# Moving a LayerNorm's mean into the block products that precede it, in a two-layer trunk kernel

## The reference

```python
proj = h @ P['o_w_in'][oi]
bg, cg, xi = proj[..., :512], proj[..., 512:1024], proj[..., 1024:1536]
uv = jax.nn.gelu(proj[..., 1536:])
yc = bg * causal_dwconv(cg * xi, c_conv_w, c_conv_b)
u = uv[..., :512]
v = layernorm(uv[..., 512:], d_ln_g, d_ln_b)      # mean and variance over the 512 channels
mix = einsum('gij,nkjgc->nkigc', tril(d_spatial_w), v in chunks of 128 tokens) + d_spatial_b
yd = u * mix
x = x + gate * (concatenate([yc, yd]) @ P['o_w_out'][oi])
```

## Time and profile before

| | |
|---|---|
| median of 3 runs | 2394.05 us (2391.03 to 2394.49) |
| profiled execution, its own time | 2396.07 us |
| span from its first to its last instruction | 2394.3 us |
| mean granted TensorE clock, of full speed | 0.991 |
| TensorE busy | 2335.9 us (98%) |
| VectorE, ScalarE, GpSimd busy | 1349.8, 749.9, 841.3 us |

### The profile page before, as it was taken

The page is one execution under the profiler, slowest core; times in us unless marked ns, Lnnn a source line. Parts: engine busy times, 40 slices in busy tenths (PEclk is TensorE's granted clock), DMA queues, the critical chain, the costliest instruction groups (busy, mean ns, idle before and its releaser), DMA issues.

```text
span 2394.3 us, 41414 instructions
## 1 busy us (share of the span) xinstructions
PE 2335.9 (98%) x17335; PEld 2223.6 (93%) x17335; DVE 1349.8 (56%) x2663; ACT 749.9 (31%) x1200; POOL 841.3 (35%) x685
## 2 busy tenths in 40 slices
PE   7999999999999999999999999899999999999998
PEld 5997888579999999999999999899999999999998
DVE  5367743466645555445546774556655555544556
ACT  5222234426322222222224523334422222222224
POOL 3221111213344433433333446522444333443341
PEclk9999999999999999999999999999999999999999
DMA  9424343971221222222221211311233434344111
GB/s 309 170 69 134 110 148 102 304 236 36 71 89 56 86 71 80 80 89 86 74 89 54 109 54 50 139 37 36 75 128 124 142 131 145 128 145 145 54 54 73
DMA packets 164566, 258.06 MB, mean 108 GB/s; under 512 B 6228, under 2 KB 150889, under 8 KB 162718
## 3 DMA queue, kind: packets, MB, share of 16 engines
q1 hardware_dynamic: 151370, 187.98, 23.6%
q0 software_dynamic: 4752, 63.28, 7.7%
q10 hardware_dynamic: 8260, 4.15, 0.6%
HBM read 232.36 MB, written 66.86 MB: 125 GB/s over the span
## 4 chain that ended last, share of the span: by engine, by line
PE 76%; DVE 2%; ACT 1%; issue 0%; POOL 0%; ACTq 0%; DVEq 0%
PE ps L3163 24%; PE ps L3192 13%; PE ps L3193 13%; PE ps L3194 13%; PE ps L3359 4%; PE ps L3313 3%; PE ps L3425 2%; PE ps L3511 1%; PE ps L3382 1%; PE ps L3705 0%; DVE tmp L2741 0%; POOL w_slot L2958 0%; DVE h_lo L2363 0%; PE ps L3544 0%; DVE x L2138 0%
## 5 line engine op out<-in xcount | busy, mean ns | idle before, releaser
L2949 POOL TENSOR_TENSOR w_slot<-w_raw,w_slot 128x512 fp32r<-128x512 f32 x272 | 358.7, 1350 | 603.0 <-DVE w_sum L2327 547.7
L3163 PE MATMUL ps<-f_hi,w_slot 128*128 128x352 f32 x1920 | 467.4, 323 | 0.0
L3192 PE MATMUL ps<-h_hi,w_slot 128*128 128x264 f32 x1536 | 437.6, 285 | 0.0
L3193 PE MATMUL ps<-h_lo,w_slot 128*128 128x264 f32 x1536 | 436.5, 284 | 0.0
L3194 PE MATMUL ps<-h_hi,w_slot 128*128 128x264 f32 x1536 | 435.2, 283 | 0.0
L2221 DVE SCALAR_TENSOR_TENSOR x<-ps,mod,x 128x704 f32<-128x704 f32 x368 | 259.2, 746 | 238.3 <-PE ps L3163 227.3
L2958 POOL TENSOR_TENSOR w_slot<-w_sum,w_slot 128x512 fp32r<-128x512 f32 x192 | 248.7, 1329 | 282.9 <-ACT w_slot L1756 282.9
L3163 PE MATMUL ps<-h_hi,w_slot 128*128 128x352 f32 x1296 | 343.3, 331 | 0.3 <-ACT sig L1607 0.3
L3163 PEld LDWEIGHTS ps<-f_hi,w_slot 128*128 128x128 f32 x1920 | 333.7, 188 | 4.1 <-issue 4.1
L3163 PE MATMUL ps<-f_lo,w_slot 128*128 128x352 f32 x960 | 307.8, 321 | 0.0
L3194 PEld LDWEIGHTS ps<-h_hi,w_slot 128*128 128x128 f32 x1536 | 289.5, 189 | 0.0
(11 more groups left out here) (467 smaller groups left out, 4017.8 us busy)
## 6 DMA issues: line engine op xcount, KB each, us to landing
w_raw<-in_ada_w SPq DMA_DIRECT2D x48, 1024.0 KB, 5.4
w_raw<-in_ffn_w_gate_up SPq DMA_DIRECT2D x44, 1024.0 KB, 5.1
out_kv_sample<-in_cache_b_kv POOLq DMA_DIRECT2D x8, 4088.0 KB, 18.4
w_raw<-in_ffn_w_down SPq DMA_DIRECT2D x22, 1024.0 KB, 4.8
w_raw<-in_e_w_in SPq DMA_DIRECT2D x11, 1024.0 KB, 5.5
w_raw<-in_o_w_in SPq DMA_DIRECT2D x10, 1024.0 KB, 5.1
cache<-in_cache_b_kv SPq DMA_DIRECT2D x16, 512.0 KB, 6.3
out_kv_sample<-in_cache_b_kv POOLq DMA_DIRECT2D x8, 1016.0 KB, 6.1
```

Source lines behind the costliest of these rows:

```text
L2949: pool.tensor_tensor(w_slot[slot_of(it.raw)][:, c], w_raw[it.raw.slot][:, c], w_slot[it.hi[0]].bitcast(F32)[:, c], ALU.subtract).then_inc( ...
L3163: mm = pe.matmul(big(t)[:, b, 0:BLK], wt, xt[:, k, b * BLK:b * BLK + BLK], start=(k == 0 and n == 0), stop=(k == K - 1 and n == 2))
L3192: pe.matmul(bank(it, j), w_high, x_high, start=first, stop=False, skip_group_check=True)
L3193: pe.matmul(bank(it, j), w_high, x_low, start=False, stop=False, skip_group_check=True)
```

## The change

The sum over v's tiles moves from unit 7 to the head of unit 6, into the tile `conv_c`; the mean matmul moves into half 1 of unit 6, behind its fourth group, and goes to the two misc banks in three parts; subtraction and squares go to unit 7, the first squares' sum between its two combinations, the others behind them. The variance matmul also goes to the misc banks in three parts, ahead of the second halves of tiles 0 and 1. As `conv_c` lies where the high part of the first half's input (`mix_hi[0]`) was, that input is kept in float32 in the meantime (`mix_kept`) and is split in unit 7; its low part is now made by VectorE, and that of the second half (`mix_lo[1]`) by GpSimd. In unit 0, VectorE makes the weight sums of unit 1 after the first combination. The tiles of the output projection are taken in their natural order, `fetch_x` brings x back in two pieces (the second when the variance matmul is done), and `splits(0, 1)` stands ahead of tile 6.

```diff
@@ mixer()
         for i, it in enumerate(units):
+            if i == 6:
+                items.append(Item("ln_sum", which="d", nt=4))
+            elif i == 7:
+                items.append(Item("ln_centre", of=mean, nt=4))
             sums_split(it)
+            if i == 7:
+                items.append(Item("mid_split", slot=0, m=0))
             items.append(Item("products", of=it, which=0))
...
             if i + 1 < len(units):
-                split(units[i + 1])
+                split(units[i + 1], sums=i > 0)
...
             if i == 4:
-                items.append(Item("mid_split", slot=0))
+                items.append(Item("mid_keep"))
+            elif i == 6:
+                mean = Item("ln_mean", which="d", nt=4, misc=take("misc", 3))
+                items.append(mean)
             elif i == 7:
-                items.append(Item("ln_sum", which="d", nt=4))
+                items.append(Item("mid_split", slot=0, m=1))
+                items.append(Item("ln_squares", nt=4))
             items.append(Item("products", of=it, which=1))
@@ spatial()
-        items.append(Item("ln_mean", which="d", nt=4, big=take("big")))
+        items.append(Item("d_fetch"))
+        items.append(Item("ln_sq", which="d", nt=4))
         t0 = first_half(0)
         t1 = first_half(1)
-        items.append(Item("ln_sq", which="d", nt=4))
+        items.append(Item("ln_var", which="d", nt=4, misc=take("misc", 3)))
         second_half(0, t0)
+        items.append(Item("ln_scale", which="d", nt=4))
         second_half(1, t1)
-        items.append(Item("ln_var", which="d", nt=4, big=take("big")))
         tile(2)
...
         mixes(0, 1)
+        splits(0, 1)
         tile(6)
-        splits(0, 1)
         mixes(2, 3)
@@ VectorE, combined()
                 for r in PAIRS:
+                    if r == 0 and it is mixes[0]:
+                        weight_sums(mixes[1], 0)
+                        weight_sums(mixes[1], 1)
+                    elif r == 0 and it is mixes[-1]:
+                        d_square_sum(1)
@@ ScalarE, mix_finish()
                     if after < len(mixes):
                         copy_mix_p1(mixes[after], r)
+                    elif r:
+                        act.wait_ge(*product_done(it, 5, 0))
+                        for m in range(2):
+                            act.activation(mix_hi[1][:, m, :], gate_c[:, m, :], ACT.Copy).then_inc(mixed_hi, 1)
@@ TensorE, seven_products(), half 1
                     of_sums(2, 3, tokens(4, B1[1]))
+                    if it is mixes[6]:
+                        pe.wait_ge(ln_sum, 4)
+                        mean_in_parts(mean_d.misc, d_total)
                     pe.wait_ge(*combined_at(it, 1, U2_MADE))
@@ TensorE
+            def mean_in_parts(q, src):
+
+                for b in range(3):
+                    misc_slot(q + b)
+                    pe.matmul(misc(q + b)[:, 0:BLK], mean_w, src[:, b * BLK:b * BLK + BLK], start=True, stop=True).then_inc(misc_ready, 1)
```

More of the change, by code:

```diff
@@ L541, in seven, with split @@
         return Item("seven", weights="ffn_w_gate_up", col=col, role=role, layer=layer, j=g, n=take("seven"), tset=2 * layer)
-    def split(it):
+    def split(it, sums=True):
         it.r = take("part")
         items.append(Item("split", of=it))
-        for half in range(2 if it.kind == "seven" else 0):
+        for half in range(2 if it.kind == "seven" and sums else 0):
             items.append(Item("w_sums", of=it, which=half))
@@ L1537, in _ @@
                     load_unit(mix_downs[1].unit + 1)
-                elif it.kind == "ln_mean" and it.which == "d":
-                    sp.wait_ge(big_ready, it.big + 1)
-                    fetch_x(7, 8, x_loaded[2])
+                elif it.kind == "ln_var" and it.which == "d":
+                    sp.wait_ge(misc_ready, it.misc + 3)
+                    fetch_x(4, 8, x_loaded[1])
                 elif it.kind == "products" and it.which == 0:
@@ L2439, in x_rooted, with d_square_sum @@
                                   ALU.mult).then_inc(xr_made, 1)
[L2441 to L2452, removed]
+            def d_square_sum(m):
+                dve.wait_ge(ln_sq, 2 + m + 1)
+                dve.wait_ge(ln_sqsum, m)
+                dve.tensor_tensor(d_sq[:, 0, :], d_sq[:, 0, :], d_sq[:, m, :], ALU.add).then_inc(ln_sqsum, 1)
             for it in plan:
@@ L2762, in _ @@
                 elif it.kind == "mix_tile" and it.which:
-                    if it.m in (0, 3, 7):
-                        dve.wait_ge(x_loaded[{0: 1, 3: 0, 7: 2}[it.m]], 32)
+                    if it.m % 4 == 0:
+                        dve.wait_ge(x_loaded[it.m // 4], 32)
                     evacuate_tile(it.big, MIX_M[it.m], it.of.layer, it.of.gate)
-                elif it.kind == "mid_split" and it.slot:
-                    for m in range(2):
-                        dve.wait_ge(mixed_hi, 7 + m)
-                        ins = low(mix_lo[1][:, m, :], mix_hi[1][:, m, :], gate_c[:, m, :])
-                    ins.then_inc(mixed_ready, 1)
+                elif it.kind == "mid_split" and it.slot == 0:
+                    dve.wait_ge(mixed_hi, 7 + it.m)
+                    ins = low(mix_lo[0][:, it.m, :], mix_hi[0][:, it.m, :], mix_kept[:, it.m, :])
+                    if it.m:
+                        ins.then_inc(mixed_ready, 1)
+                    else:
+                        own(ins)
                 elif it.kind == "sample_in":
@@ L3057, in _ @@
                     split_lo(it.k)
-                elif it.kind == "mid_split" and it.slot == 0:
+                elif it.kind == "mid_split" and it.slot:
                     for m in range(2):
-                        pool.wait_ge(mixed_hi, 5 + m)
-                        ins = pool.tensor_tensor(mix_lo[0][:, m, :], tmp[:, m, :], mix_hi[0][:, m, :].bitcast(F32), ALU.subtract)
+                        pool.wait_ge(mixed_hi, 9 + m)
+                        ins = pool.tensor_tensor(mix_lo[1][:, m, :], gate_c[:, m, :], mix_hi[1][:, m, :].bitcast(F32), ALU.subtract)
                     ins.then_inc(mixed_ready, 1)
```

102 lines of the change are left out of this document (61 added, 41 removed).

## The result

The changed kernel takes 2381.0 us (median, 2380.4 to 2383.5), the kernel before took 2393.1 beside it (2391.0 to 2394.5): a ratio of 0.9950, with a 95% interval from 0.9938 to 0.9962. Measured again beside the experiments, the ratio was 0.9944 (0.9929 to 0.9960). It is faster by about 12 us, where 11 were forecast. The profiled execution took 2381.14 us, with a span of 2379.4.

A forecast was written before the change was run, and what follows sets the result against it. TensorE, busy 98% of the span, bounds the kernel, so only its waits and slow clock can be won. Terms 1.85 + 0.45 + 1.35 + 4.2 + 2.65 + 1.05 - 0.6 = 10.95 us give 2383.1 us, range 2380.0 to 2388.0.

The forecast's parts named there:

- Unit 0: Unit 0's first combination starts earlier, so TensorE's wait goes (2.25 us); later low parts in unit 1 cost 0.4 us.
- Unit 7: TensorE's old wait in unit 7, counted as 0.65 us, shrinks to 0.2 us; bounds 0 and 1.5.
- the rival of a wait that moves there: VectorE's added work delays unit 7's combinations; waits of 1.5 to 2.5 us, 2386.7 to 2389.7 us; chance 0.11.
- Slot: TensorE's 1.2 us wait before a first half, its slot held by the mean, ends: 1.35 us.
- Variance: TensorE's stall before the variance matmul, 4.9 us start to start, shrinks to 0.7 us (range 0 to 1.4).
- The rival of a second long stall: The variance stalls TensorE again, about 4 us, perhaps with clock loss; 2386.1 to 2388.8 us; chance 0.16.
- Clock: The half-speed stretch of TensorE behind the variance's long wait goes with that stall: 2.65 us.
- Tile 7: TensorE's 0.9 us wait before output tile 7 goes, counted as 1.05 us.
- Parts: Mean and variance, each in three parts on two banks, wait for ScalarE to empty the first: 0.3 us each.
- The rival of clock lost to short gaps: Gaps from the mean and variance in parts lower TensorE's clock once, 2.65 us: 2385.8 us; chance 0.04.
- The rival of a slower kernel: The mean inside unit 6 holds up TensorE; from 15.8 us on the kernel is slower, 2398.9 us; chance 0.04.

The follow-up runs named there:

- the kernel with one copy: The changed kernel with one extra ScalarE copy between the sum of the squares and the variance product; 2383.7 us, ratio 0.9960 to the kernel before.

## Why the prediction was right

From SyncE's fetch ahead of unit 0 to the one behind the stage the two first profiles differ by (1608.58 - 1366.02) - (1593.84 - 1362.43) = 11.15 us, forecast 10.95. The second profile of the changed kernel gives the same 231.41 us, the two other profiles of the kernel before 242.61 and 241.48, so the gain is 10.1 to 11.2 us, and the clock behind the variance makes the difference. By its terms, for the first two profiles:

- *Unit 0*, forecast 2.25 - 0.4 = 1.85: measured 1.71, and 1.92 alone. The wait at the fourth group is gone whole, and the low parts cost 0.35 us in unit 1, start to start.
- *Unit 7*, 0.65 - 0.2: the fifth group follows without a gap, so the whole 0.65. The narrow working (1529.6 against 1529.7) came out on the good side, with 0.4 us to spare: the first combination's first row, at line 2313, was done at 1524.13, the fifth group began at 1524.53; the rival of a wait that moves there did not occur.
- *Slot*, 1.35: the two first halves follow unit 7 without a gap, 1.34 by the rows.
- *Variance*, 4.9 - 0.7: 4.9 - 0.61. The reason given, VectorE's two last sums beside GpSimd, is shown by the run that held GpSimd still; the sums ended 5.7 us behind the combination, inside the bounds of 2.5 to 6.3, and the upper end of 1.4 us was not reached. The row that the bounds lean on the earlier trace rows is not an addition, as the prediction calls it, but VectorE's multiplication of u by the mixing result; it too reads two SBUF tiles. The rival of a second long stall did not occur; it was nearer than I had it, since putting the variance one first half earlier is enough to bring it.
- *Clock*, 2.65: right for the profile that it was read from (2.65), but not a constant. With the same wait of 4.7 us four profiles of the old order give 2.65, 2.67, 1.75 and 1.54. As a term it should have been 1.5 to 2.7.
- *Tile 7*, 1.05: 0.98, by the run with the splits put back.
- *Parts*, -0.6: 0.29 for the mean and 0.42 for the variance, -0.71.

Together 1.71 + 0.65 + 1.34 + 4.29 + 2.65 + 0.98 - 0.71 = 10.91; 0.24 of the 11.15 are not placed.

The step that does not hold up is a reason and not a number: I took the clock to be safe because a wait of 2.1 us in unit 0 had left it at 1.00. One such row shows that a wait of this size can be free, not that it is. The two other profiles of the kernel before have the same row, waits of 2.08 and 2.13 us with 1.00 behind them, so this wait was free three times out of three. Even so a wait of 1.57 us, with 0.4 a little behind it, cost 1.5 us in one profile and nothing in another of the kernel with one copy. The conclusion stood because the longest wait left is 0.5 us; had the variance come 1 us later than forecast, the clock might have gone as well, and the forecast of 0.7 to 1.4 us for the stall should have carried that risk. The rival of clock lost to short gaps of the products in parts did not occur: 1.00 in every window here. The Trainium skill's case of such gaps (TensorE: Matmul & The Clock Gate, "A second HAM failure mode: psum-queue depth-cycling") is not shown by any run. The rival of a slower kernel did not occur either: the mean held TensorE for 1.80 us in unit 6.

The median fell by 12.1 us in the first comparison and the profiled times by 14.9. Of the 14.9, 3.3 us had arisen before 690 us, where both programs are the same; that is variation between executions and no gain.

## What to carry to other kernels

Price a stall of TensorE as two terms, its length and the clock behind it, and give the second a range: here it was 0 for waits of 2.1 us in unit 0 and for one of 1.6 at the variance, and about 1 to 2.7 us for others from 1.6 to 6.1 us, with no clear growth with the length. So the step from a wait of half a microsecond to one of two can cost as much again as the wait itself, and a product that waits on a chain should stand behind the longest independent work that its banks allow. Where VectorE's last additions on such a chain run beside GpSimd, count each at its own time plus a whole GpSimd instruction, or move one engine's work away.

## What the runs showed of the hardware

- The granted clock depends on more than the code: the kernel with one copy kept 1.00 in one profile and had 0.50 in another, with waits equal to 0.01 us.
- Most of the spread between executions arises early. SyncE's fetch of `w_raw` for `ffn_w_down` near 690 us, in code that no kernel here changes, was issued at 689.40 us in the first profile of the kernel before, 686.12 in that of the changed kernel, and from 684.18 to 692.96 over all profiles: 8.8 us, nearly as much as the change gains. Most of it is the clock. Added up over windows of 5 us from 0 to 695 us, as far as TensorE worked in them, what the granted clock lacks to full speed is worth 14.8 us in the first profile of the kernel before and 11.9 in that of the changed kernel, 2.9 of the 3.3 us between them. The earliest profile has 9.0 us, the three latest 16.4 to 19.4. Single windows go either way: 500 to 600 us has 0.95 before and 0.98 after, 400 to 500 us 0.97 and 0.95.

What makes an execution fall on the one side or the other was not found out.
